# Between the expert blocks and the value projection: buffers, load times and the order of tiles

## The chip, the cores and the metric

The kernel runs on one core of a Trainium2 chip. The metric is the device time in microseconds (us) of one execution. Three runs of the kernel before gave 2645.3 (median), 2644.18 and 2649.97.

## What is computed

The reference chains two transformer blocks on x of 1024 rows (S) by 1024 columns (D), all in float32. The first has latent (MLA) and differential attention and a routed mixture of 32 experts, two per row. The second begins with a layer that has forgetting attention (q, k, v, a forget logit per head, a gate). The change lies where the first block ends and the second begins:

```
ys = silu(xb @ w_gate[e]) * (xb @ w_up[e]) @ w_down[e]   # per block of 128 sorted rows
moe[token] += ys * weight                                # two expert rows per token
x = x + gate2 * moe
h = rms_norm(x, final_norm_g)                            # output of the first block
u = rmsnorm(h, norm_a_g)
q, k, v, f_logit, gate = split(u @ w_in_a)               # v is columns 2D to 3D
```

## The kernel before, in words

Five engines run their own instruction streams and meet through semaphores: TensorE (PE) multiplies and transposes, VectorE (DVE), ScalarE (ACT) and GpSimd (POOL) work elementwise, SyncE (SP) issues DMAs. A float32 product is made of three float32r products: each operand is split into a high part (a rounded copy) and a low part (the rest), and `split_product` (L475 to L481) issues high by high, high by low and low by high. ScalarE makes most of the high parts, VectorE the low parts. T is 8, tiles of 128 rows; KD is 8 chunks of 128 of the contraction; HALF is 512 columns, a bank of PSUM. On-chip memory has twelve slots of 16 KB per partition; `m.at(name, slot, shape, kib=...)` places a buffer in one, so buffers of different stages share bytes.

**Experts** (`phase_experts`, L2700). The blocks b = 0 to n - 1 of 128 gathered rows are run in a block loop whose upper bound is fixed and whose bodies are skipped from b = n on; in the profiled run n is 32. TensorE does gate, up and down products of 24 matmuls each. The down product's two halves are copied out of PSUM by ScalarE (`y_copy`, and `closing` for the last block) to the buffer ys, and GpSimd scatters ys to `y_dram` with an indirect DMA (`send`). Before it sends a block, GpSimd waits in `landed` until the scatter before it is in memory. `closing` waits until ys is free, and makes two casts of the value weights wv0 to their high part ahead of each of its copies.

**Tail of the same block** (`mix_and_projection`, L2118), one function per engine:

- Per tile t: the y tile holds the token's two expert rows, y0(t) and y1(t), and the x tile the residual. ScalarE scales y0 by the first weight (`scale`, L2310). VectorE runs `mix`: `combine` (L2457, adds y1 times the second weight), `gate` (L2460), `add` (L2464, onto x), `times` (L2468). ScalarE sums the squares of x and of the product (`sum_x` L2314, `sum_xg` L2319). VectorE forms two variances, ScalarE their roots, VectorE refines the reciprocals (`variances`, `refine`). ScalarE writes the scaled row into y1 (`roots`, L2325) and the block's output h into the x tile (`keep`, L2328).
- TensorE transposes the scaled row in eight pieces into PSUM (`turn_rows`, L2623), ScalarE and VectorE take the high and low parts of them (`high` L2333, `low` L2497) into uTh and uTl.
- `values(s)` is the product of one tile and one half of the value columns, 24 matmuls. The list `VUNITS` gives the order of the 16 units: in pairs of tiles, first half of both tiles, then second half of both. TensorE turns tile t + 2 ahead of need at the places in L2643 to L2647. ScalarE copies each unit to one of four stage buffers (`value_out`, L2340) and SyncE stores it to DRAM.
- y and x tiles have three buffers each (NB). SyncE reloads a y buffer behind the turn and the keep of the tile that was in it; its queue is one list (L2230 to L2302), in which a waiting DMA holds back all behind it.
- Behind the values come the forget-gate product (f_mm, 48 matmuls), the q and k groups (`group`, `group_hi`, `group_lo`) and the output gate.

wv0 is loaded when the last up product is done (u_mm), wv1 when the last down product is done (d_mm). ScalarE's tail starts with a wait for `y_landed`, which GpSimd raises when the last scatter is in memory, because wvh1 lies in the slot of ys.

Far ahead, in the in-projection (`in_projection_steps`, L610), VectorE adds squares of the latent columns (`latent_add`, L783) behind the rope of chosen units; ADD_AT (L644) names the units, and TensorE's latent sums (L885) wait for the second add.

Of the kernel before, what the change touches and what calls it, by code (L numbers as in the profile page):

```python
# [17 lines left out]
P = 128  # L18
S = 1024
D = 1024  # L20
# [589 lines left out]
def in_projection_steps(nc, A, env, sem, first):  # L610
# [33 lines left out]
    SQUARE_AT, ADD_AT, SUM_AT = (10, 11, 12, 13), (12, 15), 17  # L644
# [1473 lines left out]
def mix_and_projection(nc, A, env, sem, n_of, y_out, u_mm, d_mm):  # L2118
# [3 lines left out]
    y = [m.at("y_0", 2, [P, 2, D]), m.at("y_1", 10, [P, 2, D]), m.at("y_2", 10, [P, 2, D], kib=8)]  # L2122
    x = [m.at("x_0", 2, [P, D], kib=8), m.at("x_1", 2, [P, D], kib=12), m.at("x_2", 11, [P, D], kib=12)]
# [5 lines left out]
    wv = [m.at(f"wv{i}", 6 - i, [P, KD, HALF]) for i in range(2)]  # L2129
    wvh = [m.at(f"wvh{i}", 8 - i, [P, KD, HALF], F32R) for i in range(2)]  # L2130
# [4 lines left out]
    stage = m.at("v_stage", 9, [P, 4, HALF])  # L2135
    wf, wfh = m.at("wf", 9, [P, KD, P], kib=8), m.at("wfh", 9, [P, KD, P], F32R, kib=12)
# [10 lines left out]
    y_landed, scaled, x3, xg, squares3, var, root3, rstd3, step3 = (  # L2147
        sem("y_landed"), sem("y_scaled"), sem("x3"), sem("x3_gain"), sem("x3_sq"), sem("x3_var"), sem("x3_root"),
# [4 lines left out]
                               [sem(f"wvl{i}") for i in range(2)])  # L2153
    wf_in, wf_hi, wf_lo, f_mm = sem("wf_in"), sem("wf_hi"), sem("wf_lo"), sem("f_mm")
# [13 lines left out]
    VUNITS = [(2 * q + t, i) for q in range(T // 2) for i in range(2) for t in range(2)]  # L2168
# [30 lines left out]
    def on_sync(sp):  # L2199
        rows = env.y_dram[0:2 * S, :].rearrange("(k s) d -> s k d", k=2)  # L2200

        def y_tile(t):
            if t >= NB:
                sp.wait_ge(ut_ready, KD // 2 * (t - NB + 1))
                sp.wait_ge(h_done, t - NB + 1)
            sp.dma_start(y[t % NB][:, :, :], rows[t * P:(t + 1) * P, :, :]).then_inc(y_in[t % NB], 16)
# [40 lines left out]
        v_tile(0)  # L2247
        y_tile(4)
        x_tile(4)
        v_tile(1)  # L2250
        h_tile(2)
        v_tile(2)
        y_tile(5)
        x_tile(5)
        h_tile(3)
        v_tile(3)
        y_tile(6)
        x_tile(6)
        for s in range(4, 6):
            h_tile(s)  # L2260
            v_tile(s)
        v_tile(6)
        y_tile(7)
        x_tile(7)
        for s in range(7, 10):
            v_tile(s)
        h_tile(6)
        h_tile(7)
# [3 lines left out]
        for s in range(10, 2 * T):  # L2272
            v_tile(s)
# [30 lines left out]
    def on_pool(pool):  # L2304
        pool.sem_inc(y_landed, 1)

    def on_act(act):
# [13 lines left out]
        def roots(t):  # L2321
            act.wait_ge(var, t + 1)
            nc.scalar.activation(row_stats(t, 4, 2), row_stats(t, 2, 2), ACT.Sqrt).then_inc(root3, 1)
            act.wait_ge(rstd3, t + 1)
# [39 lines left out]
        roots(1)  # L2364
        scale(2)
        high(1)
        keep(1)
        value_out(0)
        sum_x(2)
        sum_xg(2)  # L2370
        roots(2)
        value_out(1)
        scale(3)
        keep(2)
        value_out(2)
        high(2)
        sum_x(3)
        sum_xg(3)
        roots(3)
        value_out(3)  # L2380
        high(3)
        keep(3)
        for q in range(2, T // 2):
            for t in (2 * q, 2 * q + 1):
                scale(t)
                sum_x(t)
                sum_xg(t)
                roots(t)
                keep(t)
                value_out(4 * (q - 1) + t - 2 * q)  # L2390
# [1711 lines left out]
```

## Time and profile before

| | us |
|---|---|
| median of three runs | 2645.3 |
| the profiled execution | 2645.47 |
| its span, first to last instruction | 2643.7 |
| last down product ends | 1385.7 |
| first transpose of the value stage | 1413.25 |
| value stage ends | 1527.7 |

Times in rows count from the span's start. "Idle before" is the time for which the engine had nothing to run ahead of the instruction, and the name behind the arrow is what released it. The granted clock is TensorE's, as a share of full speed: 1.00 is 2.4 GHz and 0.50 is 1.2 GHz. Matmul durations overlap: one of 128x512 is shown with 0.39 us, while a new one starts each 0.23 us.

### The profile page before, as it was taken

What the parts mean: (1) busy time and instruction counts of PE and PEld (TensorE: products, weight loads), DVE (VectorE), ACT (ScalarE), POOL (GpSimd) and SP (SyncE); (2) the same over time, 40 slices, a digit from 0 to 9 for tenths busy, and PEclk for the clock granted to TensorE, in tenths of its full rate; (3) what the DMA queues carried; (4) which work ended last, traced back from release to release, by engine and by line L of the source; (5) the groups of instructions that cost most, each with busy time, mean ns of one, the idle gap of its engine ahead of it and who ended that gap; (6) DMA issues with size and microseconds to landing.
All of it is one profiled execution on the core that took longest, in us unless ns stands there. A gap on an engine that the chain in (4) does not pass through costs nothing. (4 is left out here: it accounts for less than half of the span.)

```text
span 2643.7 us, 38257 instructions
## 1 busy us (share of the span) xinstructions
PE 2487.3 (94%) x13514; PEld 1990.1 (75%) x13526; DVE 1651.1 (62%) x3032; ACT 1374.9 (52%) x2424; POOL 380.6 (14%) x501
## 2 busy tenths in 40 slices
PE   6999999999978999999995999998999899998999
PEld 6778489888856888888874778885666688886667
DVE  5683455787567899999976545421665546742851
ACT  3353244697237788888875532322666523322850
POOL 0221022231202111111110000000232200000330
PEclk9999999999988999999997999998999999999999
DMA  6642000002049999999976411033010222113111
GB/s 245 185 135 83 0 1 1 1 15 98 20 161 403 392 421 414 412 411 418 413 275 232 153 40 65 25 128 135 33 65 33 97 88 72 32 53 134 70 49 48
DMA packets 129277, 400.26 MB, mean 151 GB/s; under 512 B 12119, under 2 KB 62556, under 8 KB 116718
## 3 DMA queue, kind: packets, MB, share of 16 engines
q1 hardware_dynamic: 117290, 359.79, 36.0%
q0 software_dynamic: 10736, 38.30, 3.6%
q8 instruction: 90, 1.47, 0.2%
q14 instruction: 53, 0.43, 0.1%
q10 hardware_dynamic: 1108, 0.27, 0.0%
HBM read 347.93 MB, written 50.40 MB: 151 GB/s over the span
## 5 line engine op out<-in xcount | busy, mean ns | idle before, releaser
L3199 DVE CUSTOM_DVE_ANT_0 fox_l<-PS,fox_c 128x1024 f32<-128x1024 f32 (+7 forms) x128 | 92.1, 756 | 120.7 <-PE PS L3246 87.0
L3136 ACT ACTIVATE fox_l<-fox_l,stat 128x1024 f32<-128x1024 f32 (+7 forms) x128 | 98.4, 771 | 90.9 <-DVE stat L3199 90.0
L3148 POOL COPY pad<-stat 128x128 f32<-128x128 f32 x64 | 18.6, 291 | 618.1 <-DVE stat L3207 617.9
L479 PE MATMUL PS<-wehu,xsTh 128*128 128x512 f32 x256 | 104.7, 409 | 0.0
L479 PE MATMUL PS<-wqkh,uTh 128*128 128x512 f32 x256 | 103.5, 404 | 0.0
L479 PE MATMUL PS<-wehg,xsTh 128*128 128x512 f32 x256 | 100.3, 392 | 2.0 <-ACT xsTh L2858 2.0
L481 PE MATMUL PS<-wehu,xsTl 128*128 128x512 f32 x256 | 101.3, 396 | 0.0
L481 PE MATMUL PS<-wqkh,uTl 128*128 128x512 f32 x256 | 100.7, 394 | 0.0
L480 PE MATMUL PS<-wqk_rest,uTh 128*128 128x512 f32 x256 | 100.5, 393 | 0.0
L481 PE MATMUL PS<-wehg,xsTl 128*128 128x512 f32 x256 | 100.2, 391 | 0.0
L481 PE MATMUL PS<-wehd,aTl 128*128 128x512 f32 x248 | 96.5, 389 | 0.0
L479 PE MATMUL PS<-wehd,aTh 128*128 128x512 f32 x248 | 96.5, 389 | 0.0
L479 PE MATMUL PS<-hTh,winh 128*128 128x512 f32 x208 | 85.5, 411 | 4.7 <-DVE hT_rest L381 3.0
L1499 DVE TENSOR_REDUCE stat<-PS 128x1 f32<-128x1024 f32 x64 | 78.1, 1224 | 17.8 <-PE PS L1536 14.3
L3223 PE MATMUL PS<-mats,fox_l 128*128 128x128 f32 x576 | 83.9, 283 | 4.3 <-DVE fox_pt L3185 1.8
L480 PE MATMUL PS<-hT_rest,winh 128*128 128x512 f32 x208 | 83.3, 401 | 0.0
L481 PE MATMUL PS<-hTh,win_rest 128*128 128x512 f32 x208 | 83.1, 400 | 0.0
L3246 PE MATMUL PS<-ka,qa 64*128 64x512 f32 (+3 forms) x384 | 83.0, 538 | 0.0
L2922 DVE TENSOR_TENSOR we0d_rest<-we0d,wehd 128x1024 fp32r<-128x1024 f32 x64 | 74.1, 1220 | 10.9 <-ACT wehd L2847 10.9
L3223 PEld LDWEIGHTS PS<-mats,fox_l 128*128 128x128 f32 x576 | 62.3, 142 | 22.6 <-issue 14.7
L3266 PE MATMUL PS<-fox_pt,va 128*64 128x128 f32 x1152 | 77.0, 278 | 0.6 <-DVE fox_pt L3185 0.6
L2922 DVE TENSOR_TENSOR we0g_rest<-we0g,wehg 128x1024 fp32r<-128x1024 f32 x64 | 74.1, 1220 | 5.2 <-ACT wehg L2847 4.1
(611 smaller groups left out, 7520.0 us busy)
## 6 DMA issues: line engine op xcount, KB each, us to landing
we0g<-in_w_expert_gate SPq DMA_DIRECT2D x16, 2048.0 KB, 11.0
we0u<-in_w_expert_up SPq DMA_DIRECT2D x16, 2048.0 KB, 9.7
we1g<-in_w_expert_gate SPq DMA_DIRECT2D x16, 2048.0 KB, 11.0
we1u<-in_w_expert_up SPq DMA_DIRECT2D x16, 2048.0 KB, 9.5
we0d<-in_w_expert_down SPq DMA_DIRECT2D x16, 2048.0 KB, 10.5
we1d<-in_w_expert_down SPq DMA_DIRECT2D x16, 2048.0 KB, 10.3
wada_rest<-in_w_ada SPq DMA_DIRECT2D x16, 1024.0 KB, 6.7
X<-in_x SPq DMA_DIRECT2D x16, 512.0 KB, 8.4
```

The source lines that it names most:

```text
L479: nc.tensor.matmul(out, lh, rh, start=start, stop=False)
L480: nc.tensor.matmul(out, lh, rl, start=False, stop=False)
L481: return nc.tensor.matmul(out, ll, rh, start=False, stop=stop)
L1499: nc.vector.reduce_max(nb[:, w % 4:w % 4 + 1], bank(w), AX_X, negate=True).then_inc(nb_ready, 1)
L2922: nc.vector.tensor_tensor(piece(wl[j][kind], kind, i), piece(w[j][kind], kind, i), piece(wh[kind], kind, i).bitcast(F32), ALU.subtract).th ...
L3136: nc.scalar.activation(prob(p, e)[:, 0:K], prob(p, e)[:, 0:K], ACT.Exp, bias=nbm[:, u % 8:u % 8 + 1], scale=-1.0, accum_out=rsum[:, u % 16 ...
L3148: nc.gpsimd.tensor_copy(rx(p).rearrange("p (e d) -> p e d", e=2), rsum[:, at:at + 2].unsqueeze(2).to_broadcast([P, 2, HD])).then_inc(rx_re ...
L3199: nc.vector.tensor_tensor_reduce(out=prob(p, e)[:, 0:K], in0=PS[:, 2 * e:2 * e + 2, :].rearrange("p a b -> p (a b)")[:, 0:K], in1=C[:, h % ...
L3223: last = nc.tensor.transpose(PS[:, 4 + at % NTB, (k % 4) * P:(k % 4 + 1) * P], prob(v, e)[:, k * P:(k + 1) * P], env.ident)
L3246: last = nc.tensor.matmul(PS[:, 2 * e + n, 0:N], env.qa[r, c, t * P:(t + 1) * P], env.ka[r, c, n * HALF:n * HALF + N], start=(n != d), sto ...
L3266: last = nc.tensor.matmul(PS[e * HD:(e + 1) * HD, 7, (w % 2) * P:(w % 2 + 1) * P], env.va[:, k, h * HD:(h + 1) * HD], PT[:, w % 2, e, k, : ...
```

## The change

What it does:

- The last block's result goes to its own buffers `ys_last` and `idy_last`; `closing` no longer waits for ys, and makes two casts of wv0 before the first copy and none between the copies. VectorE makes the other two high parts of wv0 itself (`value_hi_here`).
- SyncE issues the load of wv1 directly behind that of wv0, and the x tiles 0 and 1 when the last activations are turned (aT_t) instead of when the last down product is done.
- Buffers change slots: y, x, wv1, both wvh, the stage and the forget weights. ScalarE's tail no longer waits for GpSimd; it waits for all value stores before it writes F.
- y tile 0 is loaded in two DMAs, and VectorE scales its y0 half; the other tiles are scaled by ScalarE, one tile ahead.
- VUNITS takes both halves of a tile together, and TensorE turns tile t + 1 between the two halves of tile t. ScalarE's and VectorE's orders follow: one tile per step, with high and low of tile t - 1 inside the step of tile t.
- The second latent add moves from unit 15 to unit 14.

```diff
-    SQUARE_AT, ADD_AT, SUM_AT = (10, 11, 12, 13), (12, 15), 17
+    SQUARE_AT, ADD_AT, SUM_AT = (10, 11, 12, 13), (12, 14), 17
...
-    VUNITS = [(2 * q + t, i) for q in range(T // 2) for i in range(2) for t in range(2)]
+    VUNITS = [(t, i) for t in range(T) for i in range(2)]
...
-            sp.dma_start(y[t % NB][:, :, :], rows[t * P:(t + 1) * P, :, :]).then_inc(y_in[t % NB], 16)
+            if t:
+                sp.dma_start(y[t % NB][:, :, :], rows[t * P:(t + 1) * P, :, :]).then_inc(y_in[t % NB], 16)
+            else:
+                sp.dma_start(y0(t), rows[0:P, 0, :]).then_inc(y_first, 16)
+                sp.dma_start(y1(t), rows[0:P, 1, :]).then_inc(y_in[0], 16)
...
         sp.dma_start(wv[0][:, :, :], chunk_of(w, slice(2 * D, 2 * D + HALF))).then_inc(wv_in[0], 16)
-        sp.wait_ge(d_mm, 2 * n_of[0])
+        sp.dma_start(wv[1][:, :, :], chunk_of(w, slice(2 * D + HALF, 3 * D))).then_inc(wv_in[1], 16)
+        sp.wait_ge(aT_t, n_of[0])
         x_tile(0)
-        sp.dma_start(wv[1][:, :, :], chunk_of(w, slice(2 * D + HALF, 3 * D))).then_inc(wv_in[1], 16)
         x_tile(1)
...
+        for t in range(2, T):
+            h_tile(t)
+            v_tile(2 * t - 4)
+            v_tile(2 * t - 3)
+            if t + NB < T:
+                y_tile(t + NB)
+                x_tile(t + NB)
...
-        act.wait_ge(y_landed, 1)
         value_hi(act, 1, range(0, 4, 2))
-        scale(0)
         scale(1)
-        value_hi(act, 1, range(4, KD, 2))
         sum_x(0)
         sum_xg(0)
-        roots(0)
+        root_of(0)
+        value_hi(act, 1, range(4, KD, 2))
+        rows_out(0)
         sum_x(1)
         high(0)
         sum_xg(1)
         keep(0)
-        roots(1)
+        root_of(1)
         scale(2)
+        rows_out(1)
         high(1)
         keep(1)
...
+        for t in range(2, T):
+            if t + 1 < T:
+                scale(t + 1)
+            sum_x(t)
+            sum_xg(t)
+            if t > 2:
+                high(t - 1)
+            root_of(t)
+            rows_out(t)
+            keep(t)
+            value_out(2 * t - 4)
+            value_out(2 * t - 3)
+        value_out(2 * T - 4)
+        high(T - 1)
...
+                dve.wait_ge(y_first, 16)
+                do3(nc.vector.tensor_scalar(y0(0), y0(0), env.wts[:, 0, 0:1], None, ALU.mult))
+                dve.wait_ge(y_in[0], 16)
...
+        def value_hi_here(k):
+            nc.vector.tensor_copy(wvh[0][:, k:k + 2, :], wv[0][:, k:k + 2, :]).then_inc(vh_dve, 1)
+            dve.wait_ge(vh_dve, (k - 4) // 2 + 1)
...
+        for k in range(0, 4, 2):
+            value_lo(0, k)
+        for k in range(4, KD, 2):
+            value_hi_here(k)
+            value_lo(0, k)
         mix(0)
         combine(1)
         variances(0)
         gate(1)
         refine(0)
         add(1)
+        value_lo(1, 0)
         low(0, range(4))
         times(1)
         low(0, range(4, KD))
         variances(1)
+        value_lo(1, 2)
         refine(1)
+        value_lo(1, 4)
         combine(2)
+        value_lo(1, 6)
+        gate(2)
         low(1)
...
+        for t in range(3, T):
+            mix(t)
+            low(t - 1)
+            variances(t)
+            refine(t)
+        low(T - 1)
...
             values(s)
-            if s == 0:
-                turn_rows(1)
-            if s % 4 >= 2 and s < 2 * T - 4:
-                turn_rows(s // 4 * 2 + s % 4)
+            if s % 2 == 0 and s // 2 + 1 < T:
+                turn_rows(s // 2 + 1)
...
+    ys, ys_last = m.at("ys", 7, [P, 2, HALF]), m.at("ys_last", 10, [P, 2, HALF])
...
-                            send(bass.ds(b - 1, 1), b)
+                            send(bass.ds(b - 1, 1), b, ys_last, idy_last)
...
             def closing(b):
-                act.wait_ge(ys_free, b + 1)
+                tail["value_hi"](act, 0, range(0, 4, 2))
                 for half in range(2):
-                    tail["value_hi"](act, 0, range(4 * half, 4 * half + 4, 2))
                     act.wait_ge(d_mm, 2 * b + 1 + half)
-                    nc.scalar.copy(ys[:, half, :], PS[:, 5 + half, :]).then_inc(ys_act, 1)
+                    nc.scalar.copy(ys_last[:, half, :], PS[:, 5 + half, :]).then_inc(ys_act, 1)
```

## Rows read from the trace of the kernel before

**Rows 1.** The page, busy time of each engine in us, share of the span, instructions.
```profile
PE 2487.3 (94%) x13514; PEld 1990.1 (75%) x13526; DVE 1651.1 (62%) x3032; ACT 1374.9 (52%) x2424; POOL 380.6 (14%) x501
```

**Rows 2.** Stages: window, us; busy (x instructions) per engine; granted clock; DMA share; GB/s.
```profile
1386.00:1413.20 27.20, 0.00 (x0) 0.00 (x0) 16.61 (x21) 12.97 (x18) 0.98 (x1) 0.59 0.81 289
1413.20:1527.70 114.50, 102.10 (x448) 82.68 (x449) 64.36 (x152) 68.87 (x140) 0.00 (x0) 0.93 0.45 159
1527.70:1538.50 10.80, 10.80 (x49) 8.97 (x48) 0.00 (x0) 0.59 (x1) 0.00 (x0) 1.00 0.06 24
```

**Rows 3.** Groups of the value stage, 1413.2 to 1527.7: shapes, count, busy, mean ns, idle before.
```profile
L479 PE MATMUL PS<-wvh,uTh 128*128 128x512 f32 x128 | 52.1, 407 | 1.4 <-DVE uTl L2497 1.3
...
L2333 ACT ACTIVATE uTh<-PS,cols 128x128 fp32r<-128x128 f32 x64 | 17.5, 407 | 0.3 <-PE PS L2623 0.3
L2497 DVE SCALAR_TENSOR_TENSOR uTl<-PS,cols,uTh 128x128 fp32r<-128x128 f32 x64 | 17.4, 344 | 12.6 <-ACT uTh L2333 12.6
L2623 PE MATMUL PS<-mats,y 128*128 128x128 f32 x64 | 12.0, 336 | 38.5 <-ACT y L2325 32.8 <-DVE uTl L2497 5.5
...
L2340 ACT COPY v_stage<-PS 128x512 f32<-128x512 f32 x15 | 8.6, 587 | 4.4 <-PE PS L481 4.4
L2468 DVE TENSOR_TENSOR y<-x,rows 128x1024 f32<-128x1024 f32 x7 | 8.6, 1224 | 0.2
...
L2457 DVE SCALAR_TENSOR_TENSOR y<-y,wts 128x1024 f32<-128x1024 f32 x6 | 7.7, 1285 | 14.4 <-ACT y L2310 14.4
L2314 ACT ACTIVATE y<-x 128x1024 f32<-128x1024 f32 x7 | 7.4, 1062 | 20.4 <-DVE x L2464 20.4
...
L2310 ACT ACTIVATE y<-y,wts 128x1024 f32<-128x1024 f32 x6 | 7.1, 1178 | 0.0
```

**Rows 4.** TensorE in order of time: start, us, instruction, [idle before, releaser].
```profile
1413.25 1.97 PE L2623 MATMUL PS<-mats,y 128*128 128x128 f32 x8 [27.53 <-ACT y L2325]
...
1422.08 1.03 PE L2623 MATMUL PS<-mats,y 128*128 128x128 f32 x8
```

**Rows 5.** ScalarE in order of time, 1378 to 1405.
```profile
1382.92 2.00 ACT L2197 CAST wvh<-wv 128x1024 fp32r<-128x1024 f32 x2 [3.89 <-POOLq L2808]
...
1387.19 0.58 ACT L2882 COPY ys<-PS 128x512 f32<-128x512 f32 x1
...
1401.73 1.15 ACT L2310 ACTIVATE y<-y,wts 128x1024 f32<-128x1024 f32 x1 [3.09 <-DMA y<-y_dram]
```

**Rows 6.** VectorE in order of time, 1389 to 1403.
```profile
1389.62 4.63 DVE L2503 TENSOR_TENSOR wv_rest<-wv,wvh 128x1024 fp32r<-128x1024 f32 x4 [9.87 <-issue]
...
1402.91 1.28 DVE L2457 SCALAR_TENSOR_TENSOR y<-y,wts 128x1024 f32<-128x1024 f32 x1 [2.82 <-ACT y L2310]
```

**Rows 7.** GpSimd in order of time, and the landing times of all its scatters.
```profile
1379.48 0.99 POOL L2801 DMA_INDIRECT y_dram<-ys,idy  x1 [9.03 <-ACT ys L2875]
...
1388.57 0.98 POOL L2801 DMA_INDIRECT y_dram<-ys,idy  x1 [5.31 <-ACT ys L2882]
...
DMA to landing us min/median/max: 3.4/10.9/18.0
```

**Rows 8.** SyncE in order of time; loads of wv: count, KB each, median us to landing.
```profile
1372.50 0.40 SPq L2231 DMA_DIRECT2D wv<-in_w_in_a  x1
...
1396.30 1.40 SPq L2206 DMA_DIRECT2D y<-y_dram  x3
...
wv<-in_w_in_a SPq DMA_DIRECT2D x2, 2048.0 KB, 9.4
```

**Rows 9.** VectorE and TensorE around the latent sums of the in-projection.
```profile
163.56 0.68 DVE L852 SCALAR_TENSOR_TENSOR ropetmp<-PS,trig 128x512 f32<-128x512 f32 x1
...
165.49 1.22 DVE L785 TENSOR_TENSOR c_sq<-c_sq 128x1024 f32<-128x1024 f32 x1
...
166.76 5.26 PE L885 MATMUL PS<-ones,c_sq 128*128 128x1 f32 x32 [2.05 <-DVE c_sq L785]
```

**Rows 10.** VectorE, last low part of the first qk weights.
```profile
1524.22 1.23 DVE L2543 TENSOR_TENSOR wqk_rest<-wqk,wqkh 128x1024 fp32r<-128x1024 f32 x1 [4.21 <-ACT wqkh L2345]
```

More of the change, by code:

```diff
@@ L2128, in mix_and_projection @@
     NB = 3
-    wv = [m.at(f"wv{i}", 6 - i, [P, KD, HALF]) for i in range(2)]
-    wvh = [m.at(f"wvh{i}", 8 - i, [P, KD, HALF], F32R) for i in range(2)]
+    wv = [m.at(f"wv{i}", (6, 9)[i], [P, KD, HALF]) for i in range(2)]
+    wvh = [m.at(f"wvh{i}", (8, 5)[i], [P, KD, HALF], F32R) for i in range(2)]
     wvl = [m.rest(f"wv{i}") for i in range(2)]
@@ L2271, in on_sync @@
         group(0)
-        for s in range(10, 2 * T):
+        for s in range(2 * T - 4, 2 * T):
             v_tile(s)
@@ L2363, in on_act @@
         keep(0)
-        roots(1)
+        root_of(1)
         scale(2)
+        rows_out(1)
         high(1)
         keep(1)
[L2368 to L2390, printed above, removed]
-            value_out(4 * (q - 1) + 2)
-            high(2 * q)
-            value_out(4 * (q - 1) + 3)
-            high(2 * q + 1)
+        for t in range(2, T):
[12 more added lines that the diff above has]
+        high(T - 1)
         act.wait_ge(wf_in, 16)
         nc.scalar.copy(wfh[:, :, :], wf[:, :, :]).then_inc(wf_hi, 1)
-        act.wait_ge(h_saved[0], 48)
-        act.wait_ge(h_saved[1], 48)
         for s in range(2 * T - 4, 2 * T):
             group_hi(0, s - 2 * T + 4)
-            value_out(s)
+            if s > 2 * T - 4:
+                value_out(s)
         act.wait_ge(f_mm, 2)
         act.wait_ge(bf_in, 16)
+        for i in range(4):
+            act.wait_ge(v_saved[i], 64)
         nc.scalar.activation(F[:, 0, :], PS[0:NH, 6:8, :].rearrange("p a b -> p (a b)"), ACT.Identity,
@@ L2455, in combine @@
         def combine(t):
-            dve.wait_ge(scaled, t + 1)
+            if t:
+                dve.wait_ge(scaled, t)
+            else:
+                dve.wait_ge(y_first, 16)
+                do3(nc.vector.tensor_scalar(y0(0), y0(0), env.wts[:, 0, 0:1], None, ALU.mult))
+                dve.wait_ge(y_in[0], 16)
             do3(nc.vector.scalar_tensor_tensor(y0(t), y1(t), env.wts[:, 1, t:t + 1], y0(t), ALU.mult, ALU.add))
@@ L2517, in on_dve @@
         variances(1)
+        value_lo(1, 2)
         refine(1)
+        value_lo(1, 4)
         combine(2)
+        value_lo(1, 6)
+        gate(2)
         low(1)
-        value_lo(1, range(4, KD, 2))
-        gate(2)
         add(2)
@@ L2526, in on_dve @@
         refine(2)
-        mix(3)
-        low(2)
-        variances(3)
-        refine(3)
-        low(3)
-        for q in range(2, T // 2):
-            for t in (2 * q, 2 * q + 1):
-                mix(t)
-                variances(t)
-                refine(t)
-            low(2 * q)
-            low(2 * q + 1)
+        for t in range(3, T):
[4 more added lines that the diff above has]
+        low(T - 1)
         def group_lo(i, piece):
@@ L2735, in phase_experts @@
     route = router_steps(nc, A, env, sem)
-    tail = mix_and_projection(nc, A, env, sem, n_of, y_out, u_mm, d_mm)
+    tail = mix_and_projection(nc, A, env, sem, n_of, y_out, u_mm, aT_t)
     nc.clear_and_free_semaphores(env.spent)
@@ L2791, in fetch, with send @@
                                              ).then_inc(xs_in, 16)
-            def send(b, count):
+            def send(b, count, ys=ys, idy=idy):
                 nc.gpsimd.tensor_copy(idy[:, :], env.dest[:, b]).then_inc(idy_ready, 1)
```

54 lines of the change are left out of this document (17 added, 37 removed).

## The prediction, on record before the changed kernel was run

> **What bounds the kernel now.** I read the page's busy times first: TensorE is busy 94% of the span [rows 1], so almost all of the time is its own work, and a change that touches no product can only win where TensorE stands still. The second view is the table of stages [rows 2]. Between the last expert product and the first turned tile TensorE does nothing for 27.2 us; in the value stage behind it it is busy 102.1 of 114.5 us, at a mean granted clock of 0.93; in the forget-gate product that follows it is busy all the time. Third, the groups of the value stage [rows 3] say who is late: the turning transposes (L2623) have 38.5 us of idle time ahead of them, 32.8 behind ScalarE's scaled row (L2325), 5.5 behind VectorE's low parts. Of that, 27.5 is the one wait at the start [rows 4], so 11.0 us fall inside the stage, and 1.3 more stand ahead of L479. The fourth view, the engines in order of time around 1380 to 1403 [rows 5 to 8], gives the chain of that first wait: result copy, scatter to y_dram, reload, scale, combine, norm, transpose. Rows 9 show a separate wait, 2.05 us, far ahead in the in-projection.
>
> **The wait far ahead (ADD_AT 15 to 14).** The latent sums start at 166.76, directly behind the second latent add, which VectorE ran at 165.49 for 1.22 us, behind the rope of unit 15 [rows 9]. The rope's three operations begin at 163.56 [rows 9]; the add moves in front of them and ends at 164.8. The product before the sums ends at 166.76 - 2.05 = 164.7. So the wait shrinks from 2.05 to about 0.1: **-2.0 us**. The price is that the rope of unit 15 ends 1.2 us later. ScalarE's next evacuation waits for it, and behind that a weight cast; TensorE wants neither in the 5.3 us that the sums take nor in the 24-matmul unit behind them (5.4), so I cost it at nothing; if that cover were gone it would cost the 1.2. The squares that the add reads are done long before, so the far end is -2.05. The matmuls behind the sums could also lose some of their low-clock time, which I leave out of the sum (at most 1.6 us, eight matmuls by 0.2).
>
> **The head: from the last down product to the combine of tile 0.** Today the product ends at 1413.25 - 27.53 = 1385.7 [rows 4]. ScalarE's closing copies both sit behind pairs of weight casts of 2.0 us and the wait for the scatter before, so the second copy starts at 1387.19 and ends at 1387.77 [rows 5]; GpSimd scatters at 1388.57 [rows 7]; SyncE, which waits for that, issues the y loads at 1396.30 [rows 8], 7.7 us later. The first tile is in 5.4 us later, at 1401.73, when ScalarE scales it (1.15) [rows 5], and the combine starts at 1402.91 [rows 6].
>
> Behind the change the second copy follows the product directly (own buffer, no cast between): 1385.8 to 1386.4, and the scatter could go 0.8 later, at 1387.2. It can't if the scatter before has not landed, for GpSimd still waits for that in its own order. That one is issued at 1379.48, today behind one load of 2 MB issued at 1372.50 [rows 7, 8], and takes the shortest time of all 32, 3.4 us. Now a second load of 2 MB follows 0.4 behind the first, and the x tiles (0.5 MB each) just before the scatter. The scatters that ran beside streams of 2 MB loads have a median of 10.9 us [rows 7]. The bounds are 3.4 and 10.9 (18.0 at worst); I take 9.4, near the median, for the loads before it are many and nothing follows them: landed at 1388.9. With index copy and issue (1.0) the last scatter goes at 1389.9. This one finds the queue empty but for the rest of the x tiles: 3.4 to 7.7, I take 3.6, near the unhindered one: 1393.5. The y tile in 5.4 us gives 1398.9. Its first half lands earlier, and VectorE's multiply on it (no row has it; it is one pass over 1024 columns, so between 0.6 and the 1.29 of L2457) lies in the time that the second half takes; ScalarE's 1.15 is off the path. Combine at 1399.0 instead of 1402.91: **-3.9 us**.
>
> What else bounds this: VectorE is free for its tail only at 1389.62, behind 9.9 us without any releaser [rows 6], which I read as the rest of the block loop and expect again. It then has four low parts (4.63) and two new copies (at most 1.3 each), so it is free by 1397 at the latest, 2 us ahead of the combine. ScalarE casts the first two pairs of wv0 when it is in, 9.4 us behind 1372.5 [rows 8], and is free at 1384: the first-half copy slips past its product by 1 us at most, which GpSimd's wait hides. The later half of the wv1 casts (2.0) lie after the root of tile 0, beside VectorE's gate and refine (1.2 + 1.0); they end within 0.2 us of it. From combine to first transpose the chain stays: 1413.25 - 1402.91 = 10.3 us. Bounds of the head: with both scatters at 3.4 and VectorE next, -5.7; with 10.9 and 7.7, +1.6.
>
> The Trainium skill, page "DMA: Bandwidth & Descriptors", section "Queues, rings and completion order", says that each DMA engine alternates between the queues that have work, a packet at a time. By it the scatter at 1379.48 would share with the loads instead of queueing behind them, and would be in before 1386.4. The trace speaks against it here: median 10.9 beside loads, 3.4 without [rows 7]. By the rule the head would gain 5.3 us, not 3.9. It is a rival below.
>
> **The value stage.** Today it takes 114.5 us [rows 2]. Its need on TensorE: the first turn and first unit 1413.25 to 1422.08, 8.8 us, at the low clock at first and unchanged [rows 4]; 15 more units of 24 matmuls, each 5.4 us (48 such matmuls took 10.8 [rows 2]), 81.3; 7 more turns at 0.9 (1.03 less the overlap [rows 4]), 6.3. Sum 96.4. The question is whether ScalarE and VectorE now keep up. TensorE needs 2 x 5.4 + 0.9 = 11.75 us per tile. Per tile, with the durations of rows 3, the loop that the new order makes on ScalarE is: two sums (2.4: twice 1.06 and the reads of the sums), high of the tile before (17.5 / 8 = 2.2), wait for low, variance, root and refine on VectorE (about 1.9), scaled row, keep and scale of the next tile (three activations of L2310's form) 3.5, two value copies 1.1: 11.1 us. VectorE's loop: mix 4.96 (1.285 + 3 x 1.224), wait for the sum and high 2.2, low tail and variance 1.1, root and refine 1.9: 10.3. Both are under 11.75, because the next tile's scale is done a tile ahead and its turn happens between the two halves, so that high and low of tile t have the 5.4 us of the second half of t - 1. Today VectorE's combine waits 14.4 us in sum for that scale (L2457) and ScalarE's square 20.4 for the add behind it (L2314) [rows 3].
>
> The start has no such lead. Followed in order from the first transposes (0): turn 1 at 8.8 (scaled row ready at 8.6); second half of tile 0 at 9.7, whose four new low parts of wv1 end at 11.2 while the last is wanted at 13.9; low of tile 1 ends 14.5, wanted 15.2; turn 2 wanted 20.6, scaled row at 20.9, a stall of 0.4; low of tile 2 wanted 27.3, ready 27.7, another 0.4; from tile 3 on the lead grows by 0.65 a tile. So 96.4 + 0.8 = 97.2, and **-17.2 us**. Checked from the other side: stalls of 12.3 go, and 4.9 are matmuls and turns at the low clock behind each stall (the stage's mean is 0.93). Bounds: -18 with no stall, -8.5 if the loop takes 13 us a tile (below).
>
> Behind it: y tile t + 3 is loaded after turn t, over 14 us ahead of its scale, and lands in 5.4. The first qk weights are asked for after tile 7's halves; today their last low part ends at 1525.5 [rows 10], 13 us before the product at 1538.5 that reads them. In the new order I count 9 us of lead left. The forget product (10.8) lies between. ScalarE's four new waits for value stores stand before F, behind f_mm: nothing.
>
> Sum: -2.0 - 3.9 - 17.2 = -23.1 us against the profiled run's 2645.47 (span 2643.7), so 2622.4; the median of the runs, 2645.3, is 0.2 lower, no difference here.
>
> **Rivals.**
> 1. The scatter wait eats the head: own buffer or not, landing of the scatter before takes 10.9 and the last 7.7. Head +1.6, total 2645.5 - 2.0 - 17.2 + 1.6 = 2627.9. For it: the median; against it: the loads end soon after.
> 2. Queues share evenly: head -5.3, total 2621. The skill's rule; the row is against.
> 3. The per-tile loop is longer than TensorE's 11.75. Each hand-over between engines costs more than counted and it takes 13: 7 x 1.25 = 8.7 lost, 2631. For it: ScalarE's margin is only 0.65 a tile.
> 4. The slower side: the loop doesn't overlap at all. One buffer or store keeps scale, mix, sums, norm, row, turn, high, low, keep and two copies of a tile in one chain: 1.2 + 5.0 + 1.2 + 1.9 + 1.15 + 0.9 + 2.2 + 0.4 + 1.15 + 1.1 = 16.2 us. Stage 8.8 + 7 x 16.2 + 5.4 = 127.6, that is +13.1, with the other -5.9: 2652.7. It is slower than before from 15.4 us a tile on. Against it: three y and x buffers, and four banks for the halves.
> 5. The latent add moves its wait to the rope: 2624.4.
>
> **How the numbers follow.** Forecast 0.62, rival 1 0.13, rival 2 0.08, rival 3 0.12, rival 4 0.03, rival 5 0.02. The range reaches from the head's and stage's best (-5.7, -18, with the low-clock matmuls gone: 2618) to most of rival 3: 2617 to 2630. No change, within 0.2% or 5.3 us, about what a measurement here can tell, would need the stage to gain nothing: 0.01. Slower 0.03, faster 0.96.
>
> **What would show it.** Latent sums with no wait over 0.3 us. Wait of the last scatter's index copy on DMA, until about 1388.9 minus 2.0 (everything is 2 us earlier); y loads issued at about 1391.5; first transpose 1407.4; value stage 97 us with clock below full only in its first 4 us; two stalls of 0.4 at tile 2. Wrong if the transposes of tiles 3 to 7 wait for L2325's row, or if the stage is over 100 us, or if the gain is given back ahead of the qk product.

## The result, and the profile of the changed kernel

| | time, us | ratio to before (95%) |
|---|---|---|
| kernel before | 2644.7 (median of 4, 2639.5 to 2650.0) | |
| changed kernel | 2615.8 (median of 4, 2611.6 to 2622.5) | 0.9895 (0.9881 to 0.9908) |
| changed kernel, a second series | 2617.9 (median of 4, 2612.6 to 2619.8) | 0.9909 (0.9893 to 0.9926) |
| forecast | 2622.4 (2617 to 2630) | 0.9913 |

The first series lies 1.2 us under the range; the second, against a kernel before of 2641.8 us (7 runs), lies inside it. The profiled execution took 2617.3 us, and its span is 28.2 us shorter than that of the kernel before (2615.5 against 2643.7), in four stretches. The view is the table of windows, cut at the end of the last down product, the first turned tile, and the end of the value stage (columns as in [rows 2]). First the last stretch of the kernel before; then the busy times of the changed kernel from its page, and its four stretches:

```profile
1527.70:2643.70 1116.00, 1075.28 (x6374) 826.83 (x6384) 544.09 (x1505) 442.14 (x1028) 137.16 (x275) 0.98 0.20 69
```
```profile
PE 2481.1 (95%) x13526; PEld 1984.1 (76%) x13526; DVE 1652.0 (63%) x3035; ACT 1372.5 (52%) x2421; POOL 382.8 (15%) x501
```
```profile
0.00:1379.20 1379.20, 1306.06 (x6694) 1076.56 (x6694) 1025.68 (x1354) 850.87 (x1239) 244.10 (x224) 0.98 0.55 217
1379.20:1400.00 20.80, 0.04 (x2) 0.02 (x1) 16.42 (x23) 10.61 (x15) 1.17 (x2) 0.62 0.78 292
1400.00:1496.80 96.80, 96.73 (x448) 80.30 (x449) 65.69 (x154) 68.55 (x140) 0.00 (x0) 0.98 0.54 188
1496.80:2615.50 1118.70, 1078.29 (x6385) 827.24 (x6383) 544.22 (x1505) 442.49 (x1028) 137.58 (x275) 0.98 0.20 69
```

Ahead of the last down product 6.5 us, in the head 6.7 (27.5 less 20.8), in the value stage 17.7, and behind it 2.7 given back: 28.2. TensorE's busy time [rows 1] fell by only 6.2, so most of the gain is idle time taken away, and the value stage shows it: 448 products and turns in 96.8 us, 96.7 of them busy, at a granted clock of 0.98, against 102.1 of 114.5 at 0.93 [rows 2].

**The value stage.** Its groups in the changed kernel (shapes, count, busy, mean ns, idle before) answer to [rows 3]:

```profile
L479 PE MATMUL PS<-wvh,uTh 128*128 128x512 f32 x128 | 51.1, 399 | 0.1
...
...
L2615 PE MATMUL PS<-mats,y 128*128 128x128 f32 x64 | 9.3, 292 | 20.8 <-ACT y L2320 20.8
...
L2445 DVE SCALAR_TENSOR_TENSOR y<-y,wts 128x1024 f32<-128x1024 f32 x6 | 7.7, 1279 | 0.0
...
L2307 ACT ACTIVATE y<-x 128x1024 f32<-128x1024 f32 x7 | 7.4, 1057 | 2.3 <-DVE x L2452 2.3
```

The turns (L2615) wait once, the 20.8 of the head, and never inside the stage; ahead of L479 stands 0.1 where 1.4 stood. The 14.4 us that VectorE's combine waited for ScalarE's scale are 0.0, and ScalarE's square waits 2.3 instead of 20.4.

**The head.** GpSimd, SyncE, VectorE, ScalarE and TensorE of the changed kernel in order of time (start, us, instruction, [idle before, releaser]) answer to [rows 4 to 8]. The last down product ends at 1399.99 - 20.76 = 1379.23:

```profile
1372.99 0.99 POOL L2791 DMA_INDIRECT y_dram<-ys,idy  x1 [9.28 <-ACT ys L2865]
1380.43 0.18 POOL L2785 COPY idy_last<-dest 128x1 int32 x1 [6.45 <-DMA y_dram<-ys,idy]
1381.58 0.98 POOL L2791 DMA_INDIRECT y_dram<-ys_last,idy_last  x1 [0.96 <-POOL idy_last L2785]
...
1366.02 0.40 SPq L2237 DMA_DIRECT2D wv<-in_w_in_a  x1
1366.46 0.58 SPq L2238 DMA_DIRECT2D wv<-in_w_in_a  x1
1371.93 0.82 SPq L2217 DMA_DIRECT2D x<-x_dram  x2
1384.97 0.31 SPq L2211 DMA_DIRECT2D y<-y_dram  x1
1385.33 0.44 SPq L2212 DMA_DIRECT2D y<-y_dram  x1
...
1379.27 0.59 ACT L2871 COPY ys_last<-PS 128x512 f32<-128x512 f32 x1 [2.13 <-PE PS L481]
...
1383.13 2.36 DVE L2495 TENSOR_TENSOR wv_rest<-wv,wvh 128x1024 fp32r<-128x1024 f32 x2 [9.87 <-issue]
...
1389.14 0.75 DVE L2443 TENSOR_SCALAR y<-y,wts 128x1024 f32<-128x1024 f32 x1
1389.92 1.28 DVE L2445 SCALAR_TENSOR_TENSOR y<-y,wts 128x1024 f32<-128x1024 f32 x1
...
1399.99 1.97 PE L2615 MATMUL PS<-mats,y 128*128 128x128 f32 x8 [20.76 <-ACT y L2320]
```

The result copy no longer holds anything: it is done at 1379.86, and GpSimd still waits 0.6 us more for the scatter before, which took 7.2 us to land. The last scatter lands in 3.4 us, as the best one before did [rows 7]. At the end VectorE comes to its multiply (L2443) with no idle time at all: it has been at work since 1383.13 and is itself as late as the y tile.

**The latent sums.** They stand directly behind the product and take 3.73 us, where they waited 2.05 and took 5.26 [rows 9]. Below are the window over the sums in the kernel before, then TensorE's row and the window of the changed one; the granted clock is the third figure from the right:

```profile
166.70:172.00 5.30, 5.24 (x33) 5.24 (x33) 5.12 (x9) 3.75 (x6) 2.36 (x2) 0.69 0.87 278
```
```profile
164.61 3.73 PE L885 MATMUL PS<-ones,c_sq 128*128 128x1 f32 x32
```
```profile
164.60:168.30 3.70, 3.70 (x34) 3.69 (x34) 3.52 (x6) 1.70 (x3) 0.00 (x0) 1.00 0.65 171
```

### The profile page after: what moved, and what is told of

It reads as the page before. It is cut to its first block and busy times, and to the rows that moved or that the text cites. A ratio compares the mean times of both kernels' runs of the same rounds, so it can differ in the third digit from the quotient of the medians.

```text
span 2615.5 us, 38269 instructions
## 1 busy us (share of the span) xinstructions
PE 2481.1 (95%) x13526; PEld 1984.1 (76%) x13526; DVE 1652.0 (63%) x3035; ACT 1372.5 (52%) x2421; POOL 382.8 (15%) x501
## 5 line engine op out<-in xcount | busy, mean ns | idle before, releaser
L479 PE MATMUL PS<-wehu,xsTh 128*128 128x512 f32 x256 | 103.3, 403 | 0.0
L479 PE MATMUL PS<-wehg,xsTh 128*128 128x512 f32 x256 | 100.5, 393 | 2.8 <-ACT xsTh L2848 2.0
L479 PE MATMUL PS<-wqkh,uTh 128*128 128x512 f32 x256 | 103.1, 403 | 0.0
L479 PE MATMUL PS<-wehd,aTh 128*128 128x512 f32 x248 | 96.5, 389 | 0.0
L479 PE MATMUL PS<-hTh,winh 128*128 128x512 f32 x208 | 85.6, 412 | 4.6 <-DVE hT_rest L381 3.0
L2911 DVE TENSOR_TENSOR we0d_rest<-we0d,wehd 128x1024 fp32r<-128x1024 f32 x64 | 74.1, 1220 | 10.9 <-ACT wehd L2837 10.9
L3212 PEld LDWEIGHTS PS<-mats,fox_l 128*128 128x128 f32 x576 | 61.7, 141 | 22.9 <-issue 14.3
## 6 DMA issues: line engine op xcount, KB each, us to landing
we0g<-in_w_expert_gate SPq DMA_DIRECT2D x16, 2048.0 KB, 10.7
we0d<-in_w_expert_down SPq DMA_DIRECT2D x16, 2048.0 KB, 10.2
we1d<-in_w_expert_down SPq DMA_DIRECT2D x16, 2048.0 KB, 10.3
```

What stands on the lines that cost most here:

```text
L479: nc.tensor.matmul(out, lh, rh, start=start, stop=False)
L2911: nc.vector.tensor_tensor(piece(wl[j][kind], kind, i), piece(w[j][kind], kind, i), piece(wh[kind], kind, i).bitcast(F32), ALU.subtract).th ...
L3212: last = nc.tensor.transpose(PS[:, 4 + at % NTB, (k % 4) * P:(k % 4 + 1) * P], prob(v, e)[:, k * P:(k + 1) * P], env.ident)
```

## The experiments

Theory A is the forecast's: own buffer and early loads shorten the head, with the landing of the scatter before as the limit; the value stage wins by its order; the latent add is worth its wait. In experiment 1 alone the forecast's view is rival B there. The other theories are given with each run.

**1. The latent add alone**, in the kernel before.

```diff
-    SQUARE_AT, ADD_AT, SUM_AT = (10, 11, 12, 13), (12, 15), 17
+    SQUARE_AT, ADD_AT, SUM_AT = (10, 11, 12, 13), (12, 14), 17
```

> The kernel before with one edit, the second latent add behind unit 14 instead of 15. Theory A (the 2 us of idle time let the clock fall during the sums, and with it gone they run at full speed): latent sums with no wait, their 32 matmuls in 3.7 us instead of 5.3, the products behind them 3.8 us earlier than before, total -3.8 us or -0.14%. Rival B (as on record, the wait alone): sums still 5.3 us long, products 2.0 us earlier. Rival C (the wait moves to the rope of unit 15): nothing gained.

Measured: 2640.5 us (11 runs) against 2644.3 (17 runs), ratio 0.9990 (0.9980 to 0.9999). The sums follow the product with no wait and take 4.66 us, between rival B's 5.3 and the 3.7 that theory A expected there. The head (the wait from the last down product to the first transpose) is 27.50, as before. The edit acts alone; the medians differ by 3.9 us, but by the interval it is worth between 0.3 and 5.3 us, which doesn't tell A from B.

**2. and 3. The same pair profiled again**, because the changed kernel had come to the last down product 6.5 us earlier and the add accounts for some 2 of it. First the kernel before, unchanged, then the one of experiment 1, both on another chip.

> The kernel before, unchanged, profiled once more, to see how much of the 6.5 us by which the changed kernel's last down product ended earlier (1379.2 against 1385.7) is the edit of the latent add and how much is where the low-clock stretches of the first 1380 us happen to fall. Theory A (the edit gives 2 to 3.7 us there and chance the rest): the last down product ends between 1381 and 1386, the wait of about 2 us ahead of the latent sums is there again, and from the end of the product ahead of them to the next sums of the modulation 13.5 to 14.5 us pass. Theory B (all 6.5 us come from the change, by a mechanism not named yet): 1385.2 to 1386.2 again, and the 14.4 us too. Theory C (chance alone): under 1381, or the latent stretch under 12 us. Head wait 27.5 in all three.

> The kernel before with the second latent add at unit 14 alone, profiled once more. Theory A: the last down product ends between 1377.5 and 1382, no wait over 0.3 us ahead of the latent sums, which take 3.7 to 4.7 us, and the latent stretch takes 10.7 to 12.6 us: 2 to 3.7 less than before. Theory B (all 6.5 us come from the change): the product ends at 1377.5 to 1379.5 each time. Theory C (chance alone): anywhere from 1377 to 1386, and no better than the kernel before of the same call. Head wait 27.5 in all three.

Measured, in TensorE's order of time: before again, then the add again.

```profile
161.36 0.39 PE L481 MATMUL PS<-hTh,win_rest 128*128 128x512 f32 x1
164.17 5.63 PE L885 MATMUL PS<-ones,c_sq 128*128 128x1 f32 x32 [2.42 <-DVE c_sq L785]
...
176.56 0.95 PE L902 MATMUL PS<-ones,pad 128*128 128x1 f32 x8
1409.80 1.97 PE L2623 MATMUL PS<-mats,y 128*128 128x128 f32 x8 [27.34 <-ACT y L2325]
```
```profile
162.86 0.39 PE L481 MATMUL PS<-hTh,win_rest 128*128 128x512 f32 x1
163.26 4.29 PE L885 MATMUL PS<-ones,c_sq 128*128 128x1 f32 x32
...
175.60 0.95 PE L902 MATMUL PS<-ones,pad 128*128 128x1 f32 x8
```

I read the stretch from the end of the product ahead of the sums to the start of the next sums of one column (L902). It takes 14.8 us here (176.56 - 161.36 - 0.39), a little above theory A's 14.5, and 14.4 in the first profile of before; with the add moved 12.4 here and 12.5 in experiment 1. Over all ten profiles with the add at unit 14, those of the experiments below among them, it takes 10.6 to 12.5, mean 11.5. So the edit is worth 3.1 us on the mean, not 2.0. About 2.2 of it is wait, which goes every time. The rest is the clock, and that comes in two sizes: in six of the ten profiles the sums take 3.7 to 3.9 us and the stretch 10.6 to 11.2, in the other four, the two with this edit alone among them, 4.1 to 4.7 and 12.4 to 12.5 (the clock over the sums was 0.69 and they took 5.26 us before, 1.00 and 3.73 in the changed kernel). Why the clock holds in some and not in others is not shown.

The rest of the 6.5 is not the edit. The last down product of the kernel before ended at 1385.7 in one profile and 1382.5 (1409.80 - 27.34) in this one; with the change it ends between 1377.3 and 1381.9. Already at the end of the product ahead of the sums the run of experiment 1 was 3.8 us ahead of the first profile of before (160.91 against 164.72), and nothing is changed for TensorE up to there. From L902 to the last down product (the first profile of before has 1206.6, this one 1205.9) the ten profiles spread over 1202.9 to 1206.5. Theory B falls, C too, A holds. The 1.8 us between the means of that last stretch (1204.5 against 1206.2) stay open: with two profiles of before they can be chance.

**4. The value stage's order undone**: the changed kernel with the old order of units, turns, loads and stores.

```diff
-    VUNITS = [(t, i) for t in range(T) for i in range(2)]
+    VUNITS = [(2 * q + t, i) for q in range(T // 2) for i in range(2) for t in range(2)]
...
-            if s % 2 == 0 and s // 2 + 1 < T:
-                turn_rows(s // 2 + 1)
+            if s == 0:
+                turn_rows(1)
+            if s % 4 >= 2 and s < 2 * T - 4:
+                turn_rows(s // 4 * 2 + s % 4)
```

> The changed kernel with the value stage in its old order: both first halves of two tiles, then both second halves, the turns, sums, high and low parts, stores and reloads in the order of the kernel before. The head and the latent add stay changed. Theory A (the stage's 17.9 us come from the order alone): first transpose at about 1400 as in the changed kernel, value stage 113 to 116 us with waits of 2.5 to 5 us ahead of the turns of tiles 3, 4 and 6, total about 18 us above the changed kernel and 10 below the kernel before. Rival B (a part of it comes from buffers in other slots and from loads that are in earlier): stage under 108 us.

Measured: 2633.9 us (6 runs) against 2644.3, ratio 0.9964 (0.9952 to 0.9977). So the order is worth 16 us of the medians (2633.9 less 2617.9), or 19.4 of the value stage (116.2 less 96.8), and everything else about 10.5. The other buffer slots and earlier loads stayed in, so they don't make the stage's gain: rival B falls. Its value stage, and what TensorE waits for from 1390 on (us in total, times, longest); the 22.6 is the head:

```profile
1399.90:1516.10 116.20, 104.11 (x448) 84.02 (x449) 66.38 (x154) 69.04 (x140) 0.00 (x0) 0.93 0.46 156
```
```profile
PE PS L2649 <- ACT y L2333: 27.9, 3, 22.6
PE PS L2649 <- DVE uTl L2513: 6.1, 2, 4.0
```

**5. Scaling not ahead**: each tile's scale from tile 3 on goes back into its own tile's step (one execution).

```diff
-            if t + 1 < T:
-                scale(t + 1)
+            if t > 2:
+                scale(t)
```

> The changed kernel with ScalarE's scale of tile t made at the head of tile t's own step (tiles 3 to 7) instead of one tile ahead. Theory A (the loop of a tile is then one chain: scale 1.2, mix 5.0, sum 1.2, high 2.2, root and refine 1.5, row 1.15, keep 1.15, copies 1.1, 14.5 us against TensorE's 11.75): transposes of tiles 4 to 7 wait for the scaled row, value stage 106 to 112 us instead of 96.8, some of it at the low clock. Rival B (the look-ahead is worth little, the interleaved halves are all): stage under 99 us.

Measured: 2636.0 us. The value stage takes 114.4 us, more than the 106 to 112 expected. Its window, a group of the stage with the idle time before it, and TensorE's wait:

```profile
1404.00:1518.40 114.40, 104.65 (x448) 84.75 (x449) 66.22 (x154) 68.85 (x141) 0.00 (x0) 0.91 0.45 159
```
```profile
L2445 DVE SCALAR_TENSOR_TENSOR y<-y,wts 128x1024 f32<-128x1024 f32 x6 | 7.7, 1284 | 21.3 <-ACT y L2303 21.3
```
```profile
PE PS L479 <- DVE uTl L2485: 9.6, 4, 3.1
```

TensorE waits 9.6 us in four places. They do not lie ahead of the transposes, as expected, but ahead of the products, behind the low parts of the tile just turned. Behind three of them (of 3.1, 2.7 and 2.7 us) 13, 8 and 7 products in a row take about 0.63 us instead of 0.39, and its busy time is 104.7 instead of 96.7. One line of ScalarE's order holds the whole gain of the stage, since without it the new order is as slow as the old.

**6. The next tile turned behind both halves** instead of between them (one execution).

```diff
-            if s % 2 == 0 and s // 2 + 1 < T:
+            if s % 2 and s // 2 + 1 < T:
```

> The changed kernel with the turn of tile t + 1 behind both halves of tile t instead of between them. Theory A (the 5.4 us of the second half hide high and low of the next tile): at each of seven tiles TensorE waits 1.0 to 1.5 us for the first low part of the tile just turned, value stage 104 to 108 us. Rival B (turning between is worth nothing, order of the halves is): stage 96 to 98 us.

Measured: 2623.7 us. The stage takes 105.5, as expected; the same view's waits:

```profile
1401.00:1506.50 105.50, 99.83 (x449) 81.59 (x450) 65.76 (x154) 68.63 (x140) 0.00 (x0) 0.96 0.47 172
```
```profile
PE PS L479 <- DVE uTl L2485: 5.6, 7, 2.4
```

There are seven waits of 0.8 on the mean (expected 1.0 to 1.5) for the low parts, once a tile, and 3.1 us more busy time. The turn's place is worth 8.7 us; scale ahead and turn between are both needed, and their prices don't add up (17.6 and 8.7 of a gain of 17.7).

**7. wv1 and the x tiles issued late again**, as before, with the last result's own buffer (one execution).

```diff
-        sp.dma_start(wv[1][:, :, :], chunk_of(w, slice(2 * D + HALF, 3 * D))).then_inc(wv_in[1], 16)
-        sp.wait_ge(aT_t, n_of[0])
+        sp.wait_ge(d_mm, 2 * n_of[0])
         x_tile(0)
+        sp.dma_start(wv[1][:, :, :], chunk_of(w, slice(2 * D + HALF, 3 * D))).then_inc(wv_in[1], 16)
         x_tile(1)
```

> The changed kernel with x tile 0, the second value load and x tile 1 behind the last down product, as before. Theory A (which loads stand ahead of a scatter sets when it lands): the scatter of the block before the last lands in 3.4 us instead of 7.4, the last one is issued at the end of its copies, 0.9 us earlier than in the changed kernel, and then lands in 7 to 8 us instead of 3.4, so the y loads are issued 3 to 4 us later and the wait ahead of the first transpose is about 24 us instead of 20.8. Rival B (the own buffer is the gain, the loads' places are not): the last scatter goes earlier and lands in under 5 us, wait 20 to 21 us.

Measured: 2620.0 us, head 25.2. GpSimd's scatters and VectorE's multiply:

```profile
1375.61 0.99 POOL L2791 DMA_INDIRECT y_dram<-ys,idy  x1 [8.92 <-ACT ys L2865]
1379.20 0.18 POOL L2785 COPY idy_last<-dest 128x1 int32 x1 [2.60 <-DMA y_dram<-ys,idy]
1383.27 0.98 POOL L2791 DMA_INDIRECT y_dram<-ys_last,idy_last  x1 [3.88 <-ACT ys_last L2871]
...
1395.64 0.75 DVE L2443 TENSOR_SCALAR y<-y,wts 128x1024 f32<-128x1024 f32 x1 [3.80 <-DMA y<-y_dram]
```

The two landings change places, as theory A has it: the scatter before lands in 3.4 us and the last one in 7.9. The landing of the last scatter is the dearer one, since TensorE has no product left to run beside it and the reload waits for all of it. The early loads are worth 2.6 to 4.5 us of the head (25.2 against the 20.8 to 22.6 of the five profiles in experiment 9, mean 21.6).

**8. The last result in the shared buffer again** (one execution).

```diff
-                            send(bass.ds(b - 1, 1), b, ys_last, idy_last)
+                            send(bass.ds(b - 1, 1), b)
...
+                act.wait_ge(ys_free, b + 1)
...
-                    nc.scalar.copy(ys_last[:, half, :], PS[:, 5 + half, :]).then_inc(ys_act, 1)
+                    nc.scalar.copy(ys[:, half, :], PS[:, 5 + half, :]).then_inc(ys_act, 1)
```

> The changed kernel with the last result in the shared buffer again: its copies wait until the scatter before has landed, which GpSimd waits for anyway. Theory A (the landing is the bound and the own buffer saves only the copies behind it): copies start when the scatter has landed, at 1380.5, the last scatter is issued at about 1382.6 instead of 1381.6, wait ahead of the first transpose 21.8 instead of 20.8. Rival B (the own buffer is most of the head's gain): wait of 24 us or more.

Measured: 2617.9 us, head 22.9. The scatter before lands 8.1 us behind its issue, both copies follow it, and the last scatter goes at 1383.24, 3.6 us behind the product instead of 2.4. The head lies midway between theory A's 21.8 and rival B's 24, but most of the excess is not the buffer's: in experiment 5, which has the own buffer, the scatter before also took 8.1 us, the last one went 3.2 us behind the product, and the head was 22.3. Beside that run the own buffer is worth some 0.5 us, the copies behind the landing, which is A's mechanism.

**9. The changed kernel again**, beside experiment 10.

> The changed kernel again, to be compared with the next one on the same chip. Theory: 1.0 to 1.2% faster than the kernel before; the wait ahead of the first transpose 20.5 to 22.7 us (20.8 and, with the same head and the stage in the old order, 22.6 so far), the value stage 96.8 us again.

Measured: the second series of the table. Span 2610.8 in the profiled run, head 21.5, scatters landing in 7.2 and 3.4 again; in the window of the value stage TensorE is busy 96.7 of 96.8 us, as in the first profile. The head repeats within 0.8 us here; experiments 4, 5 and 6 change nothing ahead of the first transpose either and have 22.6, 22.3 and 20.8, so this head takes 20.8 to 22.6 us, mean 21.6. The trace shows two places that make the spread. The scatter before lands in 7.2 us in three of the five, in 7.4 and 8.1 in experiments 4 and 5. And from combine to first transpose 10.1 us pass in two of them, 10.7 to 11.7 in the other three. There ScalarE's list is the reason: the scale of tile 1, which waits for y tile 1, stands ahead of tile 0's sum. First the changed kernel, then experiment 4:

```profile
1392.71 1.15 ACT L2303 ACTIVATE y<-y,wts 128x1024 f32<-128x1024 f32 x1 [1.67 <-DMA y<-y_dram]
1393.76 1.06 ACT L2307 ACTIVATE y<-x 128x1024 f32<-128x1024 f32 x1
```
```profile
1392.88 1.15 ACT L2316 ACTIVATE y<-y,wts 128x1024 f32<-128x1024 f32 x1 [3.74 <-DMA y<-y_dram]
1393.94 1.04 ACT L2320 ACTIVATE y<-x 128x1024 f32<-128x1024 f32 x1
```

In the first the add that tile 0's sum needs ends at 1393.73, just ahead of the sum; in the second it ends at 1392.07, and the sum starts 1.9 us late, held up by the wait for a tile that it doesn't read. The scale of tile 1 behind tile 0's sums was not tried.

**10. A better head?** wv1 issued behind the scatter before the last, and ScalarE instead of VectorE makes the last two high parts of wv0.

```diff
-        sp.dma_start(wv[1][:, :, :], chunk_of(w, slice(2 * D + HALF, 3 * D))).then_inc(wv_in[1], 16)
         sp.wait_ge(aT_t, n_of[0])
+        sp.dma_start(wv[1][:, :, :], chunk_of(w, slice(2 * D + HALF, 3 * D))).then_inc(wv_in[1], 16)
...
-            value_hi_here(k)
             value_lo(0, k)
...
+                tail["value_hi"](act, 0, range(4, KD, 2))
```

Here the function's argument is the semaphore of the low parts of the last activations (a_lo) instead of that of their turns (aT_t).

> The changed kernel with two edits in the head: the second value load waits until the last low part of the activations (just ahead of the scatter before the last), and ScalarE, not VectorE, makes the other two high parts of wv0, behind its last copy. Theory A (loads queued ahead of a scatter hold it up, and the last scatter's issue is bound by that landing): the scatter before the last lands in 3.5 to 5 us instead of 7.4, the last one is issued 0.8 to 1.0 us earlier behind its copies, y loads 0.9 earlier, wait ahead of the first transpose 0.9 us shorter than in the changed kernel (about 20). Rival B (VectorE's exit from the loop binds and the landing doesn't): VectorE ready 1.4 earlier, wait shorter by up to 1.4. Rival C (the queues share evenly whatever stands ahead): no change in the landing, nothing gained by the load; total within 0.1% of the changed kernel in all cases.

Measured: 2617.2 us (4 runs), ratio 0.9902 (0.9885 to 0.9918), against 0.9909 for the changed kernel beside it (experiment 9): no difference. Head 23.2, where theory A expected about 20.

```profile
1372.29 0.99 POOL L2789 DMA_INDIRECT y_dram<-ys,idy  x1 [8.16 <-ACT ys L2863]
1380.17 0.18 POOL L2783 COPY idy_last<-dest 128x1 int32 x1 [6.89 <-DMA y_dram<-ys,idy]
...
1372.60 0.39 SPq L2239 DMA_DIRECT2D wv<-in_w_in_a  x1
...
1390.00 0.75 DVE L2443 TENSOR_SCALAR y<-y,wts 128x1024 f32<-128x1024 f32 x1 [2.93 <-DMA y<-y_dram]
```

The load of wv1 is now issued 0.3 us behind the scatter, and the scatter still takes 7.7 us. So theory A falls: it is not enough to issue the load behind it. The last scatter, issued at 1381.32 while wv1 is still coming in (until about 1382.6), takes 5.1 us instead of 3.4; the y loads are issued 7.9 us behind the product instead of 5.7. VectorE is free 1.4 us earlier (8.5 us behind the product instead of 9.9) and waits 2.9 for the y tile. Rival B falls too: of two equal limits one was relieved and the other made worse.

Not tried: to let GpSimd send the last scatter without waiting for the one before. Both write y_dram, and nothing else orders them.

## Why the forecast came out as it did

- **Value stage, -17.2: right.** It lost 17.7, and no stall of 0.4 at tile 2 appeared. The clock is low in its first 4 us (0.50) and then full, as forecast. The new order removes the waits and with them the low clock behind them, and the loops of ScalarE and VectorE do fit into TensorE's 11.75 us a tile. (Two sums of that part are slightly off: VectorE's terms add up to 10.2, not 10.3, and rival 4 is slower than before from 15.2 us a tile on, not 15.4.) Experiments 4 to 6 show the mechanism: undone, the stage is 116 us; without scaling a tile ahead 114; with the turn behind both halves 105. Rivals 3 and 4 are out.
- **Head, -3.9: the failed step.** The chain was right and one of its terms was mis-sized, the 9.4 us for the landing of the scatter before. The head gained 6.8 (6.0 in the second profile, 5.9 on the mean of the five with the same head), more than the bound of 5.7 that the range used. Relative to the last down product, the forecast has the last scatter at +4.2 us, y loads at +7.8, combine at +13.3, first transpose at +23.6. The changed kernel has +2.4, +5.7, +10.7 and +20.8. Of the 2.9 us between -3.9 and -6.8, 1.9 are one figure: "I take 9.4, near the median" for the landing of the scatter before, which took 7.2; the rest is 0.2 on the last landing, 0.6 on the y tile, whose halves are in 3.5 and 4.4 us behind their issues instead of 5.4 for the whole, and 0.2 between combine and transpose. A median of 10.9 over a stretch in which loads of 2 MB never stop [rows 7] was the wrong row for a place where two loads and two x tiles are all that is left. The bound of 5.7 was VectorE's own date, with its two new copies at 1.3 us each; they took 0.69. As for the parts of the change, the early loads are worth 2.6 to 4.5 us (experiment 7), the own buffer some 0.5 (experiment 8); the halved y tile, the scale on VectorE and ScalarE's dropped wait for GpSimd share the rest and were not undone one by one.
- **VectorE "free by 1397 at the latest, 2 us ahead of the combine": right in size, wrong in its meaning.** Behind the product it is free 9.9 us later (1389.14), and the forecast's 11.3 was an upper end. But since the scatter landed earlier than forecast, VectorE has become one of two equal limits: the y tile's halves are in at 1388.5 and 1389.7, VectorE comes at 1389.14. The 9.87 us of VectorE without a releaser came back to the hundredth [rows 6], as forecast.
- **Latent add, -2.0: too small, the second failed step.** The wait went, as said, but I had left the low clock behind it out of the sum ("at most 1.6 us"). Ten profiles against two give 3.1 on the mean, so 1.1 of clock, and up to 3.8 (14.4 to 10.6) against the first. That was a term of the sum, not a remainder.
- **Ahead and behind.** What is left of the first stretch (6.5 less 3.7, so 2.8) and the 2.7 us given back behind the stage cancel. The latter lies within the spread between runs: from the end of the last value product on, the second profile of the changed kernel takes 4.9 us less than the first (1113.6 against 1118.5), and the two profiles of before lie between them (1115.7 and 1115.8).

With the terms at their measured sizes, 2622.4 - 2.9 (head, first profile) - 1.1 (latent, on the mean) - 0.5 (stage) = 2617.9; with the head's mean of 5.9 it is 2618.8. The first series has 2615.8, the second 2617.9, the median of all eight runs is 2617.3. So of the 6.6 us by which the first series misses the forecast 3.6 to 4.5 are these terms, and 2 to 3 are spread between runs. That the second series lies inside the range is partly luck: both terms were too small there too. The range was too tight below: its low end took the head's bound, the best stage and the low clock of the latent sums, but the head went past its bound, and nothing was left for the spread of some 5 us either way that runs of this kernel show.

**The rule weighed.** The Trainium skill, page "DMA: Bandwidth & Descriptors", section "Queues, rings and completion order", has each DMA engine alternate, a packet at a time, between the queues with work; the forecast set it aside, and took queueing behind the loads. The packets of both queues, counted over two stretches behind the scatter's issue at 1372.99 in the changed kernel (queue, kind, packets, MB, share of 16 engines), decide between them. First 1373 to 1377, then 1377 to 1380.2:

```profile
q1 hardware_dynamic: 742, 1.50, 105.6%
```
```profile
q1 hardware_dynamic: 354, 0.76, 62.8%
q0 software_dynamic: 144, 0.52, 40.0%
```

For 4 us the scatter moves nothing; then it shares with the loads, in 3 us. The trace agrees with the rule for the second part: both queues move together, and between 1378 and 1379 they move 67 and 68 packets. For the first part the rule has nothing. Neither the forecast's 9.4 nor the landing within 6.9 us that it had worked out for the rule (before 1386.4) came; the 7.2 measured was nearer to the rule, and so was the head: rival 2's -5.3 lay nearer than my -3.9.

## What to carry to other kernels

Where a stage's engines are each under the bound but the stage stalls, look for a step of the next tile that sits behind this tile's chain: one line moved a tile ahead was worth 17.6 us here, with the rest of the new order in place. The other side of it: work for the next tile, placed ahead of this tile's work in one engine's list, makes this tile wait for the next one's load (in the head here by up to 1.9 us). Price a transfer by rows from the same situation (what runs beside it, and for how long yet), not by a median over another. And when a wait in front of TensorE goes, count what its clock did behind the wait as a term of its own.

## What the runs showed that I had not expected

- A scatter starts late when loads run beside it. In the kernel before, with the load queue almost empty, its packets lie 1.5 to 3.5 us behind the issue at 1379.48, and it lands in 3.4. In the changed kernel nothing of it moves for 4 us; with the load issued just behind it (experiment 10), one packet of 144 moves in 4.7 us; in experiment 7 none in 4.2. All of them then share for 3 to 4 us and land in 7.2 to 7.9 (up to 8.1 over all profiles). Full engines alone don't explain it, since the loads took only 66% of the engines' time in experiment 10. What holds the start up was not found.

```profile
q0 software_dynamic: 144, 0.52, 64.8%
```
```profile
q1 hardware_dynamic: 395, 0.79, 66.1%
q0 software_dynamic: 1, 0.00, 0.2%
```

The first is the kernel before, 1381 to 1383; the second experiment 10, 1372.3 to 1377.

- Removing a wait ahead of short products can give more than the wait. The 32 one-column sums behind the 2 us wait took 5.26 and 5.63 us; without it 3.73 to 4.66, and with the clock at 1.00 throughout 3.73.
- VectorE leaves the block loop after the same 9.87 us, counted from its last low part of the activations, in all twelve profiles, whatever stands around it; it can bound a tail and shows as idle "issue".
